# A four-layer transformer on one core: the heads of its three routed phases in another order

## The reference, cut to what matters

```python
def _layer_norm(x, g, b):
    x32 = x.astype(jnp.float32)
    mu = jnp.mean(x32, -1, keepdims=True)
    var = jnp.mean(jnp.square(x32 - mu), -1, keepdims=True)
    return ((x32 - mu) * lax.rsqrt(var + LN_EPS) * g + b).astype(x.dtype)
...
        x = _layer_norm(DEEPNORM_ALPHA * x + mix, ln1_g[i], ln1_b[i])
        ffn = _hier_moe(x, moe_w_group[i], moe_b_group[i], moe_w_expert[i], moe_b_expert[i],
                        moe_w_gate[i], moe_w_up[i], moe_w_down[i])
        x = _layer_norm(DEEPNORM_ALPHA * x + ffn, ln2_g[i], ln2_b[i])
...
def _hier_moe(x, w_group, b_group, w_expert, b_expert, w_gate, w_up, w_down):
    ...
    g_prob = jax.nn.softmax((t @ w_group + b_group).astype(f32), axis=-1)
    g_p, g_sel = lax.top_k(g_prob, 1)
    e_logits = (t @ w_expert + b_expert).astype(f32).reshape(n_tok, MOE_GROUPS, MOE_EXPERTS_PER_GROUP)
    idx = jnp.broadcast_to(g_sel[:, :, None], (n_tok, 1, MOE_EXPERTS_PER_GROUP))
    e_prob = jax.nn.softmax(jnp.take_along_axis(e_logits, idx, axis=1)[:, 0], axis=-1)
    top_p, top_i = lax.top_k(e_prob, MOE_TOP_K)
    weights = g_p * top_p / jnp.sum(top_p, axis=-1, keepdims=True)
    ...
    for e in range(MOE_EXPERTS):
        hid = jax.nn.silu(t @ w_gate[e]) * (t @ w_up[e])
        y = y + gate[:, e:e + 1] * (hid @ w_down[e])
```

## Time and profile before

| | |
|---|---|
| median of 3 runs | 2094.15 us |
| lowest, highest | 2091.66, 2096.18 us |
| profiled execution, its own time | 2094.62 us |
| its span | 2092.8 us |
| mean granted clock of TensorE | 0.998 |
| TensorE busy | 2065.8 us, 99% of the span |
| VectorE busy | 1686.7 us, 81% |
| ScalarE busy | 1413.4 us, 68% |
| GpSimd busy | 139.0 us, 7% |
| mean HBM traffic | 287 GB/s |
| chain that ended last | TensorE 90%, VectorE 6%, ScalarE 2% |

### The profile page before, as it was taken

One profiled execution on the slowest core, in us unless ns is written; L12 is line 12 of the kernel. 1 busy time (PEld: TensorE's weight loads), 2 busy tenths in 40 slices (PEclk: granted clock), 3 DMA queues, 4 the chain that ended last, 5 costly groups with the idle time before them and its releaser, 6 DMA issues.

```text
span 2092.8 us, 30682 instructions
## 1 busy us (share of the span) xinstructions
PE 2065.8 (99%) x9972; PEld 1683.9 (80%) x9972; DVE 1686.7 (81%) x2268; ACT 1413.4 (68%) x1893; POOL 139.0 (7%) x132
## 2 busy tenths in 40 slices
PE   9999999999999999999999999999999999999999
PEld 8976888768887887888867888888888888888887
DVE  5756998649997656555767999999999999999997
ACT  5754785446885544444634888888888888888886
POOL 1001000002100001111211000000000000000000
PEclk9999999999999999999999999999999999999999
DMA  8417994516994456451434999999999999999995
GB/s 294 155 68 284 403 412 163 215 77 277 411 350 151 163 239 251 181 200 40 161 141 163 393 381 388 374 383 377 382 381 376 387 371 385 378 385 379 364 403 210
DMA packets 88550, 601.59 MB, mean 287 GB/s; under 512 B 10545, under 2 KB 10609, under 8 KB 19985
## 3 DMA queue, kind: packets, MB, share of 16 engines
q1 hardware_dynamic: 79616, 569.88, 69.1%
q0 software_dynamic: 8704, 30.08, 4.7%
q10 hardware_dynamic: 144, 0.52, 0.1%
HBM read 585.12 MB, written 15.32 MB: 287 GB/s over the span
## 4 chain that ended last, share of the span: by engine, by line
PE 90%; DVE 6%; ACT 2%; issue 1%; DMA 1%; POOL 0%; DVEq 0%; SPq 0%; ACTq 0%; POOLq 0%
PE bank L532 21%; PE bank L528 21%; PE bank L529 21%; PE bank L519 4%; PE bank L521 4%; PE bank L520 4%; PE bank L1119 2%; PE bank L1595 2%; PE bank L688 1%; PE bank L3195 1%; DVE pj_lo L565 1%; PE bank L457 1%; PE bank L1671 1%; PE bank L3178 0%; PE bank L463 0%
## 5 line engine op out<-in xcount | busy, mean ns | idle before, releaser
L2027 DVE TENSOR_TENSOR gu_lo<-ffw_gu,gu_hi 128x1024 fp32r<-128x1024 f32 x620 | 754.3, 1236 | 89.2 <-ACT gu_hi L1817 75.2
L1817 ACT CAST gu_hi<-ffw_gu 128x1024 fp32r<-128x1024 f32 x620 | 649.3, 1052 | 86.8 <-PE bank L532 40.6
L528 PE MATMUL bank<-gu_lo,xg_hi 128*128 128x512 f32 x1152 | 462.4, 401 | 0.0
L529 PE MATMUL bank<-gu_hi,xg_hi 128*128 128x512 f32 x1152 | 448.8, 390 | 0.0
L2027 DVE TENSOR_TENSOR dn_lo<-ffw_d,dn_hi 128x1024 fp32r<-128x1024 f32 x293 | 357.2, 1229 | 23.4 <-ACT dn_hi L1825 14.6
L1825 ACT CAST dn_hi<-ffw_d 128x1024 fp32r<-128x1024 f32 x304 | 319.3, 1056 | 57.4 <-PE bank L532 50.1
L532 PE MATMUL bank<-gu_hi,xg_lo 128*128 128x512 f32 x1152 | 356.6, 391 | 0.0
L528 PE MATMUL bank<-dn_lo,hidt_hi 128*128 128x512 f32 x652 | 254.4, 390 | 0.7 <-ACT hidt_hi L1854 0.5
L529 PE MATMUL bank<-dn_hi,hidt_hi 128*128 128x512 f32 x652 | 253.7, 389 | 0.0
L532 PEld LDWEIGHTS bank<-gu_hi,xg_lo 128*128 128x128 f32 x1152 | 216.2, 188 | 46.5
L529 PEld LDWEIGHTS bank<-gu_hi,xg_hi 128*128 128x128 f32 x1152 | 216.9, 188 | 40.4
(11 more groups left out here) (476 smaller groups left out, 2728.4 us busy)
## 6 DMA issues: line engine op xcount, KB each, us to landing
ffw_gu<-in_gate_up_m SPq DMA_DIRECT2D x288, 1024.0 KB, 7.3
ffw_d<-in_down_m SPq DMA_DIRECT2D x144, 1024.0 KB, 8.8
pieces<-in_pieces SPq DMA_DIRECT2D x70, 1024.0 KB, 7.1
ffw_gu<-in_gate_up_ff SPq DMA_DIRECT2D x22, 1024.0 KB, 7.0
ffw_d<-in_down_ff SPq DMA_DIRECT2D x11, 1024.0 KB, 8.9
h<-token_sums POOLq DMA_DIRECT2D x3, 1024.0 KB
norm_vec<-in_ln_g POOLq DMA_DIRECT2D x4, 512.0 KB, 4.3
norm_vec<-in_ln_b POOLq DMA_DIRECT2D x4, 512.0 KB, 6.2
```

Source lines behind the costliest of these rows:

```text
L528: nc.tensor.matmul(bank, a_hi, b_lo, start=start, stop=False)
L529: nc.tensor.matmul(bank, a_hi, b_hi, start=False, stop=False)
L1817: nc.scalar.copy(gu_hi[:, 2 * k:2 * k + 2, :], ffw_gu[:, blk["slot"], 2 * k:2 * k + 2, :])\
L2027: return V.tensor_tensor(out, x, hi.bitcast(F32), ALU.subtract)
```

## The change

The change touches the heads of the three routed phases, and one waiting point of the first blocks.

- **Tile 1 turned when centered** (m0, m1). `layer_norm_center` of tile 1 writes to `row_x` and signals `h_centered`; TensorE turns tile 1 from there, without its root and shift. `layer_norm_end` reads `row_x` and writes `h` as before.
- **Root and shift on the logits.** What the turned tile lacks is put on its 20 logits: logits = root * (centered . route) + (ln1_b . route) + bias. The second term comes from 8 new products on TensorE (`shift_tensor`) with the shift vector, one column of `par_all` per chunk, as a broadcast operand; they stand where 7 fillers stood. VectorE adds the bias to it (L2476) before it waits for the logits, and then needs two operations for the logits in place of one (L2480, L2481). Two parameters of 8 columns each come into `par_all`.
- **Order on VectorE** (m0, m1): `tok_lo` of tile 1 goes from in front of the logits to behind `pick_t`; the group's values go from in front of `row_of` to behind the counts.
- **ScalarE** copies tile 1's features to `xT` before it casts tile 1 to `tok_hi`, and its scaled copy of `h` waits for tile 0's `tok_lo` alone.
- **Gather** (m0, m1): all products with `tok_hi` first, then those with `tok_lo`, as m2 had it.
- **m2:** `tok_lo` of tile 0 goes from VectorE to GpSimd, in front of tile 1's root.
- **Fillers:** 6 become 1 in front of the first block, in all three; 14 become 12 in m2.
- **First blocks:** `gate_up_tensor` with `lo_ready` makes the high products of both quarters, then waits, then makes both low ones.

The diff, cut to its core:

```diff
-    def layer_norm_center(j):
-        vlink(V.scalar_tensor_tensor(out=h[:, j, :], ...))
-    def layer_norm_end(j):
+    def layer_norm_center(j, dst=None, *done):
+        vlink(V.scalar_tensor_tensor(out=h[:, j, :] if dst is None else dst, ...), *done)
+    def layer_norm_end(j, src=None):
...
-        layer_norm_center(j)
+        if j:
+            layer_norm_center(j, row_x, sem("h_centered"))
+        else:
+            layer_norm_center(j)
...
     def turn_tile_tensor(pe, t, j):
-        tile_wait(pe, t, j)
+        src = h[:, j, :]
+        if j and t in ("m0", "m1"):
+            pe.wait_ge(sem("h_centered"), ROUTER[t] + 1)
+            src = row_x
+        else:
+            tile_wait(pe, t, j)
...
-            for x, y in roots_in[phase]:
+            for k, (x, y) in enumerate(roots_in[phase]):
+                if phase == 6 and k == len(roots_in[phase]) - 1:
+                    pool.wait_ge(sem("out_half"), 2 * T * (MIXER["da"] + 1))
+                    pool.wait_ge(sem("tok_hi_ready"), T * ROUTER["m2"] + 1)
+                    nc.gpsimd.tensor_tensor(tok_lo[:, 0, :], normed[:, 0, :], tok_hi[:, 0, :].bitcast(F32), ALU.subtract)\
+                        .then_inc(sem("tok_ready"), 1)
                 rsqrt_gpsimd(pool, x, y)
...
-            if lo_ready is not None and k == 2 * pair:
-                pe.wait_ge(*lo_ready)
-            for c in (2 * k, 2 * k + 1):
-                last = low_product(psum[st["par"]], x(c)[1], gu_hi[:, c, :], c == DC - 1)
-            last.then_inc(sem("gu_piece"), 1)
+            if lo_ready is None:
+                low_quarter(st, x, k)
+        if lo_ready is not None:
+            pe.wait_ge(*lo_ready)
+            for k in (2 * pair, 2 * pair + 1):
+                low_quarter(st, x, k)
...
+    def shift_tensor(t, route):
+        shift = par[f"ln1_b{ROUTER[t]}"]
+        for c in range(DC):
+            nc.tensor.matmul(psum[1][:, 2 * P:2 * P + route.shape[2]], shift[:, c:c + 1].to_broadcast([P, P]), route[:, c, :],
+                             start=(c == 0), stop=(c == DC - 1))
...
                 turn_tile_tensor(pe, t, j)
-                keep_busy_tensor(1, 2 if j else 7)
+                if j:
+                    keep_busy_tensor(3, 2)
+                else:
+                    shift_tensor(t, route)
...
-        keep_busy_tensor(1, 14 if t == "m2" else 7)
+        keep_busy_tensor(3, 12 if t == "m2" else 7)
...
         rows_turn_tensor(pe, t, 0)
-        keep_busy_tensor(1, 6)
+        keep_busy_tensor(1, 1)
...
+                    if j:
+                        features_tile_scalar(act, t, j)
                     tile_wait(act, t, j)
                 nc.scalar.copy(tok_hi[:, j, :], ...)
-            if t != "m2":
-                features_tile_scalar(act, t, 1)
...
+        if grouped:
+            turned_wait(dve, t, 1, 0)
+            vlink(V.tensor_tensor(logit_shift, psum[1][:, 2 * P:2 * P + cols], bias, ALU.add))
         dve.wait_ge(sem("route_logits"), ROUTER[t] + 1)
         if grouped:
-            vlink(V.tensor_tensor(logit, src, over(bias, 1, T), ALU.add))
+            vlink(V.tensor_tensor(logit[:, 0, :], src[:, 0, :], bias, ALU.add))
+            vlink(V.scalar_tensor_tensor(out=logit[:, 1, :], in0=src[:, 1, :], scalar=rstd[:, 1:2], in1=logit_shift,
+                                         op0=ALU.mult, op1=ALU.add))
...
         pick_vector(dve, t, 0)
-        if not grouped:
-            tok_lo_vector(dve, t, 1)
+        tok_lo_vector(dve, t, 1)
...
         if grouped:
+            group_values()
             best_two()
...
         rms_begin(1)
-        tok_lo_vector(dve, "m2", 0)
         normed_tile_vector(1)
```

43 lines of the change are left out of this document (22 added, 21 removed).

## The result

The changed kernel takes 2100.67 us (median of 8 executions, 2095.66 to 2108.04) against 2092.83 us of the kernel before (median of 8): a ratio of 1.0035, with an interval of 1.0024 to 1.0046. It is slower, by 0.35%. The time lies inside the range that was given, at its upper end, 3.7 us above the number forecast.

A forecast was written before the change was run, and what follows sets the result against it. VectorE's chain from logits to hidt_lo was taken to bound m0 and m1, with some slack in m2. 1.66 + 1.66 - 0.95 = +2.4 us on the profiled 2094.6 gave 2097.0 us; range 2091.5 to 2101.0.

The forecast's parts named there:

- the first rival: Heads m0 and m1: thin products let TensorE's granted clock fall; one head 2098.7 us, both 2100.3; chance 0.3.
- two falls of 1.7 us each: Clock falling in both m0 and m1, 1.7 us of full speed lost in each: 2100.3 us.
- VectorE's chain in m0 and m1, 1.66 each: Heads m0 and m1: moved tok_lo and group values make hidt_lo late, low products start 1.66 us later in each.
- The gap of 0.35: m0, VectorE's small steps before gu_lo: a gap without known releaser; m0 might cost 1.3 us, not 1.66.
- the second wait for `hidt_lo`: TensorE's waits before the change: two for hidt_lo, 0.4 us in total, read as one in m0, one in m1.
- Turning early brings nothing: m0 and m1: TensorE isn't free, so tile 1 is turned 0.06 us earlier and not 1.4.
- fillers bring nothing in m0 and m1: m0 and m1: five fillers fewer (1.1 us) start the first block earlier, but TensorE then waits for VectorE.
- m2, -0.95: Head of m2: tok_lo off VectorE and fewer fillers let the low products start 0.95 us earlier.
- POOL not in the way: m2: POOL's subtraction, 2.40 us, is covered and doesn't slow VectorE; the opposing rival, 2097.9 us, had chance 0.1.

The follow-up runs named there:

- e1_wide_shift: The changed kernel with each of the 8 shift products over 128 columns instead of 20; median 2096.13 us, ratio to before 1.0013.
- e6_group_back: e1_wide_shift with the group's values alone back in front of row_of; median 2095.63 us, ratio to before 1.0009.
- e5_cast_first: e1_wide_shift with VectorE's order of before (tok_lo, group's values) and ScalarE casting tile 1 first as before; ratio to before 0.9998.
- e9b_turn_h: e1_wide_shift with tile 1 turned from h with root and shift on it, the shift products staying as fillers; ratio to before 1.0012.
- e10b_fillers_back: e1_wide_shift with the 6 fillers in front of the first block and the old waiting point; ratio to before 1.0040.
- e12_fillers_again: The kernel of e10b_fillers_back run once more, unchanged; median 2097.49 us, ratio to before 1.0026.
- e7_all_wide: e1_wide_shift with the router's logits over 128 columns too, in all three heads; median 2095.71 us, ratio to before 1.0011.
- e2_thin_fillers: The kernel before with 8 fillers of 20 columns for the 7 of 128 behind tile 0's turn in m0 and m1; median 2098.17 us, ratio 1.0031.

## Why the prediction was right, and where it was not

The time is in the range, its side was not the likeliest: I gave 0.60 to no measurable change and 0.33 to slower. It is slower, in the way of the first rival. That it lies in the range is in part luck: the range ended at 2101.0 for two falls of 1.7 us each, the median is 0.33 us short of that, and the one profile shows a single fall in m0 and m1, of 5.36 us. Against its own base the miss is larger than 3.7 us: the forecast stood 2.9 above 2094.15, the measured time stands 7.8 above 2092.83.

- **VectorE's chain in m0 and m1, 1.66 each: right in kind and nearly in size.** 1.41 in m0 and 1.83 in m1 at the full clock (e1_wide_shift), 3.24 together for 3.32. The gap of 0.35 that I gave to the range is there: 0.50 in front of one small operation in m0 of before, gone after, and absent in m1, so m0 pays 0.35 less. e6_group_back and e5_cast_first take the terms apart: values back 0.6, the rest 0.8 and 0.85.
- **Its parts.** Logits 0.25 earlier (I had 0.38), `row_of` 0.44 (0.52), `tok_lo` then 0.69 late (0.62), the chain to `xg_lo` 1.74 late (1.67). These compare the two traces as they stand; counted from tile 0's turn, which is 0.07 earlier after, the four are 0.18, 0.37, 0.76 and 1.81, and the turn of tile 1 is 0.11 later and not 0.06 earlier. The waits of TensorE for `gu_lo` and `hidt_lo` in m0 are 0.48 and 0.74, not about 1 us each.
- **A row read wrongly.** I took the second wait for `hidt_lo` in the earlier trace rows to be m1's. It is in the dense phase, at 805.14. In m1 of before TensorE had no such wait. `hidt_lo` ended at 506.34 there and the low products started at 506.39, just when TensorE reached them, so that there was no slack either and "the same wait" did no harm to the sum.
- **Turning early brings nothing; fillers bring nothing in m0 and m1.** Both as worked out. e9b_turn_h shows the first. For the second there are the profiles of e10b_fillers_back and e12_fillers_again, and times that leave it open.
- **m2, -0.95: at the full clock -0.73.** The first low products were 0.91 earlier (31.70 in e7_all_wide, 32.61 before, both from tile 0's turn). But they now stand behind a wait of 0.36, and behind such a wait the next pair follows in 1.51 us instead of 1.36: that was left out.
- **POOL not in the way: right.** Its 2.36 and VectorE's unchanged 0.69 and 1.42 are shown above. This agrees with the rule that the prediction takes from the Trainium skill (SBUF — State Buffer, section SBUF: two separate sides).
- **The clock, the step that failed.** "4.0 x 0.42 = 1.7 us of full speed lost in a fall" and "one head: 2098.7; both: 2100.3". That a fall is what thinner products bring was right, and its chance of 0.3 was too low for what came; its price was mis-sized. I took a fall to last 4 us at most, because the two in the profile of before did. In m1 of the changed kernel the clock stayed down for 17 us, and the head cost 5.36 us beyond the order's 1.83 (41.36 less 36.00), three times my price; in m1 of e2_thin_fillers it was down for 3.4 us, and cost 1.40, which is near my price, and in its m2 for 6.8 us by the windows, and cost 2.08. Why it came back soon in one and late in the other the runs don't tell. Over the executions it costs 0.22% (1.0035 against 1.0013), 4.6 us.
- **The evidence against it was one execution.** I held the full clock in m2's head against the rival: 8-column products at 1.00. Of the eleven profiles with such thin logits in m2, seven have the clock down there. A clock that falls in some executions can't be read off one. The spread was a better sign: of 103 executions of the kernel before, those with a mean clock of 0.999 took 2092.0 us on average, those with 0.998 2094.0, those with 0.997 2095.9.
- The Trainium skill (TensorE: Matmul & The Clock Gate, What's actually happening) has the half clock as the state that activity has to lift, and by it the loss of fillers was the danger. The runs agree in so far as thinner products lowered the mean granted clock (0.9955 against 0.9990). The length of the fall is another matter: in m1 the clock stayed at 1.2 GHz through four windows in which TensorE is busy for the whole 4.00 us.
- **The chances were added wrongly.** Their parts, as listed, make 0.06 faster, 0.62 same and 0.32 slower, not 0.07, 0.60 and 0.33.

The sum by what was measured: 1.41 + 1.83 - 0.13 for the order, with m2's fall in it, is +3.1 us. e1_wide_shift, which is this and nothing else, has +0.13%, 2.7 us. The rest, up to 7.3 us, went with the width of the shift products, and so with the clock in m0 and m1; the one profile shows it in m1 alone.

## What to carry to other kernels

Find out which engine ends a stage before working on another: here TensorE was given an earlier start, and VectorE's list in front of `hidt_lo` had grown by two pieces that had been free where they stood. Taking one entry of that list out of the way, with the fillers that this made superfluous, gave 1.10 and 1.05 us, where the change had lost 1.4 and 1.8. A filler here had two jobs, to pass the time and to hold the clock; whoever replaces it by useful work must look at the second. Letting the eight shift products run over 128 columns, most of them unread, took the loss from 0.35% to 0.13%. And where the clock can fall, take several executions: one profile shows one draw.
